# Order edits and a moved cache copy in a two-layer hybrid decoder step

## The reference

```python
p   = rms_norm(x, norm_w) @ w_in          # 4480 padded columns: q, k, v, gates, indexer, ssd inputs
o_a = sparse attention, 4 heads            # a token indexer picks the top 64 (prompt) or 256 (sample) keys
o_c = dilated window attention, 6 heads    # (128, 1), (512, 4), (2048, 16)
y_b = Mamba-2 SSD, 6 heads                 # conv width 4, state 128, gated RMSNorm
h   = x + concat[o_a * silu(g_a), o_c * silu(g_c), y_b] @ w_out
```

## Time and profile before

| | us |
|---|---|
| median of 3 runs | 581.45 (580.13 to 587.98) |
| the profiled execution, whole | 580.49 |
| its span, first to last instruction | 578.8 |
| PE busy | 556.2 (96% of the span) |
| DVE busy | 356.7 |
| ACT busy | 175.9 |
| POOL busy | 238.1 |

### The profile page before, as it was taken

One profiled execution on the slowest core, in us unless ns is written; L12 is line 12 of the kernel. 1 busy time (PEld: TensorE's weight loads), 2 busy tenths in 40 slices (PEclk: granted clock), 3 DMA queues, 4 the chain that ended last, 5 costly groups with the idle time before them and its releaser, 6 DMA issues.

```text
span 578.8 us, 13517 instructions
## 1 busy us (share of the span) xinstructions
PE 556.2 (96%) x4694; PEld 389.3 (67%) x4694; DVE 356.7 (62%) x1090; ACT 175.9 (30%) x458; POOL 238.1 (41%) x430
## 2 busy tenths in 40 slices
PE   8999999999999999999999999999999999999994
PEld 7776655676777656667677665657777766666763
DVE  4864655676786796443257564757688678854322
ACT  4013521202323524641101252321123282464210
POOL 1405642449323756361111375314873175634200
PEclk9999999999999999999999999999999999999998
DMA  8979999999996999998969999999999699999993
GB/s 339 365 261 313 370 367 381 417 359 357 375 379 201 353 359 387 345 353 291 396 214 384 294 371 368 372 403 410 330 370 383 245 334 354 387 367 312 322 395 122
DMA packets 75253, 198.39 MB, mean 343 GB/s; under 512 B 11601, under 2 KB 44530, under 8 KB 71090
## 3 DMA queue, kind: packets, MB, share of 16 engines
q1 hardware_dynamic: 53138, 98.32, 48.0%
q0 software_dynamic: 21472, 98.03, 46.1%
q10 hardware_dynamic: 576, 1.18, 0.6%
HBM read 189.33 MB, written 52.00 MB: 417 GB/s over the span
## 4 chain that ended last, share of the span: by engine, by line
PE 72%; DMA 13%; DVE 8%; ACT 2%; issue 2%; SPq 2%; POOL 0%; DVEq 0%; POOLq 0%; ACTq 0%
PE bank L962 69%; DMA kv<-in_kk 5%; DMA w<-in_w 4%; PE bank L1022 3%; DMA kv<-in_vv 3%; DVE phased L2017 1%; DVE phased L2020 1%; SPq L439 1%; DMA x<-in_x 1%; ACT shared L751 1%; DVE xw L2035 1%; DVE xn L2290 1%; ACT srow L878 1%; DVE shared L1811 0%; DVE shared L1826 0%
## 5 line engine op out<-in xcount | busy, mean ns | idle before, releaser
L962 PE MATMUL bank<-xn,w 128*128 128x288 f32 x1120 | 291.6, 414 | 0.0
L962 PEld LDWEIGHTS bank<-xn,w 128*128 128x128 f32 x1120 | 205.4, 190 | 68.4 <-issue 14.2
L439 POOL DMA_DIRECT2D kv<-in_kk x128 | 68.8, 538 | 88.3 <-issue 42.0
L439 POOL DMA_DIRECT2D kv<-in_vv x128 | 68.8, 538 | 84.5 <-issue 43.8
L704 ACT ACTIVATE pt<-bank 128x288 f32<-128x288 f32 x48 | 19.6, 409 | 177.7 <-PE bank L962 177.5
L962 PE MATMUL bank<-pt,w 128*128 128x288 f32 x256 | 64.8, 409 | 1.9 <-DMA w<-in_w 1.8
L962 PEld LDWEIGHTS bank<-pt,w 128*128 128x128 f32 x256 | 47.9, 191 | 16.8 <-DMA w<-in_w 3.9
L542 POOL DMA_DIRECT2D out_keep<-in_buf x48 | 24.9, 525 | 69.4 <-PE bank L962 67.5
L1722 DVE TENSOR_SCALAR_CACHE_REDUCE hit<-sc,tb 128x516 bf16<-128x516 f32 x62 | 46.5, 750 | 2.2
L962 PE MATMUL bank<-kv,pt 128*32 128x256 f32 x512 | 33.2, 384 | 1.9 <-DMA kv<-in_vv 1.9
L962 PE MATMUL bank<-kv,qz 128*32 128x256 f32 x512 | 34.3, 385 | 0.0
(11 more groups left out here) (272 smaller groups left out, 747.7 us busy)
## 6 DMA issues: line engine op xcount, KB each, us to landing
w<-in_w SPq DMA_DIRECT2D x86, 512.0 KB, 8.4
out_keep<-in_buf POOLq DMA_DIRECT2D x16, 2044.0 KB, 13.5
kv<-in_kk SPq DMA_DIRECT2D x128, 160.0 KB, 8.4
kv<-in_kk POOLq DMA_DIRECT2D x128, 160.0 KB, 5.8
kv<-in_vv SPq DMA_DIRECT2D x128, 128.0 KB, 5.7
kv<-in_vv POOLq DMA_DIRECT2D x128, 128.0 KB, 5.3
kv<-in_dil SPq DMA_DIRECT2D x16, 576.0 KB, 11.7
kv<-in_dil POOLq DMA_DIRECT2D x16, 576.0 KB, 8.5
```

The lines of the kernel that those rows point to most:

```text
L439: engine.dma_start(kv[:, s, r * rec:(r + 1) * rec], a["kk" if what == "page" else "vv"][bass.ds(page + layer * N_POOL, 1)].rearrange("o p ...
L962: return pe.matmul(out, lhsT, rhs, start=start, stop=stop, skip_group_check=True, **k)
```

## The change

It has four parts.

1. In layer 0 the first norm's three `sum_squares` stand behind `proj(1)` and no longer behind `proj(0)`.
2. On VectorE the last two `top8_round(1)` move behind `inverse_group(0)` and `state_out(4)` to `state_out(7)`, in both layers.
3. On TensorE `proj(33)` stands ahead of value group 20, and on SP the weight load that waits for tile 33 stands ahead of the load that waits for group 20, in both layers.
4. `keep` takes a tuple of transfers. Of sequence 4 of each layer the 2044 KB transfer is issued on its own behind tile 25; its two small ones stay in the output stage. The other copies there move up: in layer 0 sequence 5 from `out4` to `out0`, in layer 1 sequence 6 from `out0` to tile 34. Number and bytes of all copies stay the same.

```diff
 COPY_ROW = 9344
-FRONT_KEEPS = ((), ((0, 6, "proj1"), (0, 7, "proj4")))
-STAGE_KEEPS = (((0, 0), (0, 1), (0, 2), (0, 3)), ((1, 0), (1, 1), (1, 2), (1, 3)))
-OUTPUT_KEEPS = (((0, 4, "out0"), (0, 5, "out4")), ((1, 4, "proj34"), (1, 5, "proj34"), (1, 6, "out0"), (1, 7, "out1")))
+WHOLE, SMALL, LARGE = (0, 1, 2), (0, 1), (2,)
+FRONT_KEEPS = ((), ((0, 6, WHOLE, "proj1"), (0, 7, WHOLE, "proj4")))
+STAGE_KEEPS = tuple(tuple((L, b, LARGE if b == 4 else WHOLE) for b in range(5)) for L in range(DEPTH))
+OUTPUT_KEEPS = (((0, 5, WHOLE, "out0"), (0, 4, SMALL, "out5")),
+                ((1, 5, WHOLE, "proj34"), (1, 6, WHOLE, "proj34"), (1, 7, WHOLE, "out1"), (1, 4, SMALL, "out1")))
...
-                for i, (lo, hi) in enumerate(((0, 6), (6, 9), (9, 12), (12, 18), (18, 21), (21, 26))):
+                for i, (lo, hi) in enumerate(((0, 6), (6, 9), (9, 12), (12, 18), (18, 20), (20, 26))):
                     consumed(*RING[48 + lo:48 + hi])
                     next_w(29 + i)
...
-                def keep(layer, b, use):
+                def keep(layer, b, groups, use):
 
                     pool.wait_ge(filled(use), nth(L, use))
-                    for g in range(3):
+                    for g in groups:
...
                 masked(0)
                 masked(1)
+                keep(*STAGE_KEEPS[L][4], "proj25")
                 consumed(*RING[40:44])
...
                 for i in range(6):
                     proj(i)
-                    if i == 0:
+                    if i == (1 if L == 0 else 0):
                         if L == 0:
                             sum_squares(0, KT - 3)
                         sum_squares(L, KT - 2)
...
                 dilated_values(0)
+                proj(33)
                 value_groups(20, 21)
-                proj(33)
...
                 prompt_state_out()
-                for n in range(2):
-                    top8_round(1)
                 inverse_group(0)
                 for b in range(4, NB):
                     state_out(b)
+                for n in range(2):
+                    top8_round(1)
                 prompt_mask(1)
```

More of the change, by code:

```diff
@@ L553, in consumed @@
                         after(pool, POOL, L, item)
-                for layer, b, use in FRONT_KEEPS[L]:
-                    keep(layer, b, use)
+                for layer, b, groups, use in FRONT_KEEPS[L]:
+                    keep(layer, b, groups, use)
                 for u in range(NPAIR):
@@ L646, in _ @@
                 consumed(*RING[64:])
-                for layer, b, use in OUTPUT_KEEPS[L]:
-                    keep(layer, b, use)
+                for layer, b, groups, use in OUTPUT_KEEPS[L]:
+                    keep(layer, b, groups, use)
                 for name in ("ki_out", "feat_out", "tail_out", "h_out"):
```

## The result

The changed kernel took 575.05 us (median of 4 runs, 573.20 to 579.35) against 580.95 of the kernel before (4 runs), a ratio of 0.988 with an interval of 0.984 to 0.993: **1.2% faster**, clear of noise and short of 2%. In two later comparisons the same kernel gave 0.989 (0.982 to 0.997) and 0.993 (0.990 to 0.996), so the gain is 0.7 to 1.2%. The ratios leave out runs of the kernel before that are counted as slow, over 1.5% above its fastest, so they are not quotients of the medians given here.

The account below looks back on a forecast made before the run. DMA and TensorE (busy 556.2 of 578.8 us) were taken as both almost full. Order gains of 4.1 us less copy losses of 0.9 and 1.5 gave 1.7 us faster, 579.7 us, range 576.4 to 583.4.

Parts of the forecast that it names:

- First norm's sums: Start of layer 0: the 1.13 us wait becomes 0.5 us before tile 3; gain 0.9 us, bounds 0 to 1.4.
- the pace of VectorE's multiplications: First norm, layer 0: 0.47 us per multiplication, so tile 3 starts near 20.8 us.
- Rounds of top values: Both layers: TensorE's two waits for the last `state_out` go; gain 1.07 + 1.14 us, bounds 1.6 to 2.2.
- Value page 20: Layer 0 only: group 20's 1.75 us wait goes, 0.76 us returns at the turn behind it; gain 1.0 us.
- The copy behind tile 25: Holes before the value loads: the copy overruns them, delaying the first six groups; loss 0.9 us layer 0, 1.5 layer 1.
- move 310 GB/s: 2044 KB are 2.09 MB, 6.75 us: Holes behind tile 25: the copy's DMA cost at the lone-copy rate, against 5.5 and 5.0 us free.
- Rival (a): Holes take the copy whole, all order gains stay: 577.3 us, or 575.6 with output stage relief; chance 0.25.
- Relief of the output stage: Gain from 2044 KB less in each output stage: taken as 0, other end 1.8 us.
- one copy is what layer 1 keeps: Layer 1's output stage: one copy stays, as ahead of layer 0's 0.48 us weight wait, so relief 0.
- The sum: Whole kernel: 0.9 + 1.07 + 1.14 + 1.0 - 0.9 - 1.5 = 1.7 us faster, so 579.7 us.
- The order edits: First norm's sums, rounds of top values and value page 20 together: gain 4.1 us.

Follow-up runs that it names:

- rounds_only: The kernel before with only the two rounds of top values moved behind the state updates; 580.45 us, one run.
- double: The changed kernel with the 2044 KB copy of sequence 5 moved behind tile 25 as well; 590.62 us, ratio 1.012 (1.006 to 1.018).
- bytes_out1: The kernel before with the three edits of order, and the copies behind out0 moved to out1; 577.95 us, ratio 0.994 (0.990 to 0.997).
- sums_only: The kernel before with only the first norm's sums moved behind tile 1; 584.00 us, one run.
- late: The changed kernel with the same 2044 KB copy issued some 18 us later, ahead of loads for value groups 5 and 7; 593.69 us, ratio 1.016.
- l1_out0: The changed kernel with the last whole copy of layer 1 issued behind out0, no longer behind out1; 580.36 us, one run.
- order_only: The kernel before with the three edits of order alone, copies as before; 577.63 us, ratio 0.990 (0.986 to 0.994).

## Why the prediction was wrong

**First norm's sums: right, a little small.** 1.15 us for 0.9. The step that failed is the pace of VectorE's multiplications, 0.38 us and not 0.47: in the trace of before each waited some 0.03 us for TensorE to free its step of `xn`, so that they kept TensorE's pace, one in 0.48 us.

**Rounds of top values: right.** Both waits went. How much of the 2.2 us reached the end of the kernel is not shown; the next page wait, at group 20 of layer 1, was 1.78 us in `rounds_only`, and it can be as long without this part.

**Value page 20: right for layer 0.** 1.75 us gone, 0.81 come back. That layer 1 gains nothing was read from a trace in which its group 20 happened not to wait.

**The copy behind tile 25: the mechanism right, the size wrong, and with it the sign.** The failed step is "move 310 GB/s: 2044 KB are 2.09 MB, 6.75 us". 310 GB/s is the rate of a copy running alone; a share of 1.00 went with it there, and 1.03 with 426 GB/s in the changed kernel (170 to 176), so the share does not tell how much more the engines can move. Beside the loads in the hole the copy cost 4.4 us of share in the 10 us window, 5.0 by its packets, against 5.5 and 5.0 free. Instead of 2.4 us lost it was nothing measurable. The trace of before had the better price: of its sixteen such copies the fifteen beside other transfers cost 5.1 to 6.0 us by their packets, and only the lone one 6.5; that puts the copy at the edge of the holes, not over a microsecond behind it. The rate of other mixed traffic would not have served, since it depends on what is mixed: just ahead of the hole (171 to 174) it was 420 GB/s at a share of 1.02, behind it 324 at 1.01. Rival (a) was the true case, and `double` shows how near its edge lies: one more such copy costs 5.5 us in layer 0 and 4.8 in layer 1.

**Relief of the output stage: taken as 0, was 1.35 us in layer 1.** The failed step is "one copy is what layer 1 keeps". It counted copies and bytes and passed over the place, one tile later. The argument that bytes alone change nothing was right: `bytes_out1` has more bytes and no wait. These are waits in traces; in the medians the relief could not be seen.

**The sum.** By the traces, VectorE's last group of instructions starts at 571.78 before and at 565.46 after, 6.3 us earlier. In waits over 0.15 us: 1.1 at the start, 2.2 at L2020, 1.75 at group 20, 1.35 at layer 1's weights, 0.2 at group 5, less 0.65 at the turns, 0.6 at page pairs and 0.3 at layer 0's weights: 5.1. TensorE's busy time makes up 1.4, 556.2 before and 554.8 after with as many instructions, and gaps under 0.15 us take 0.2 back. The same matmuls being busy for less is luck of this trace more than the change: in the two other traces of the changed kernel, with spans of 574.1 and 574.7, it is 556.1 and 555.9. The last 1.0 of the span's 7.3 us falls behind the final writes; the stretch from VectorE's last group to the end was 7.0 us before, 6.0 after, and I don't know why.

**The one trace.** The profiled run of before took 580.49 us, but the same kernel gave medians of 582.25 to 585.58 us beside the experiments, with single runs up to 589.13 among those that the ratios use. TensorE's waits on pages and weights vary by several microseconds: in `sums_only` they are 12.3 us in all, in the traced run of before 6.0. A sum worked out from one good trace sees few of the waits that an edit guards against. The order edits, forecast at 4.1 us, measured 5.9 (3.5 to 8.2) alone; how much of that comes this way stays open.

## What to carry to other kernels

Price a bulk transfer for a hole in DMA by what such transfers cost the engines beside other traffic in that trace, not by the rate of a lone copy, and then compare it with the hole's free share to the microsecond: here one copy was free, and of the second nearly each microsecond beyond the edge was one of TensorE's. Where loads are needed in a burst, issue the bulk copy behind the last of them, not between them; the place was worth some 1 us of waits a layer where 2 MB less were worth nothing. Whether such a wait shows in the time is another matter, with run times that scatter by several microseconds. And before a wait in one trace is priced, see whether a second trace of the same code has it.

## What the runs showed that I had not expected

**The granted clock falls behind a stall.** `double` and `late` lost more than their waits: the span of `double` is 16.7 us over that of the changed kernel's first trace (13.5 to 14.1 over those of the other two), with 10.3 us of waits for value pages. TensorE's busy time is 561.3 us, 6.5 more for the same instructions. Its windows, columns as in the earlier trace rows:

```profile
190.00:196.00 6.00, 4.10 (x35) 2.27 (x33) 3.99 (x15) 5.98 (x18) 2.95 (x6) 1.00 1.07 360
196.00:202.00 6.00, 1.97 (x20) 0.63 (x21) 4.52 (x17) 0.87 (x2) 2.56 (x5) 0.64 1.06 358
202.00:206.00 4.00, 4.00 (x21) 2.16 (x22) 0.00 (x0) 0.00 (x0) 1.73 (x4) 0.50 1.07 366
206.00:210.00 4.00, 4.00 (x17) 2.73 (x15) 0.00 (x0) 0.00 (x0) 2.15 (x4) 0.76 1.07 345
```

TensorE was busy 4.10 of 6 us, then 1.97 of 6, and the granted clock went from 1.00 to 0.50, the 1.2 GHz level; two value groups took 1.94 us there and 1.07 at the full clock. It came back between 206 and 210.

A fall needs no wait of that length. In `l1_out0`, behind the 2.71 us wait that ends at 206.43, and in `order_only`, behind one of 1.16 us that ends at 512.37, the windows show:

```profile
208.00:212.00 4.00, 4.00 (x11) 2.84 (x11) 1.49 (x1) 1.57 (x2) 0.00 (x0) 0.58 1.06 352
514.00:518.00 4.00, 4.00 (x29) 3.21 (x32) 0.46 (x2) 2.85 (x4) 0.00 (x0) 0.58 1.06 369
```

A mean of 0.58 over 4 us is up to 1.7 us lost. In the kernel before, the window from 232 to 236, behind its 1.75 us wait, has a granted clock of 1.00. So a DMA wait can cost more than its length, and its length alone does not tell whether it will.

**Equal code, unequal landings.** The weight waits of layer 0 with the same copy behind out0 were 0.76, 1.01 and 1.76 us in three traces of the changed kernel; those at group 20 of layer 1 were 0, 1.07 and 0.
